# Decay and value-rate mixing factors applied to the low-rank weights, and the opening norm in two groups of two tiles

## What is computed

```python
def rms_norm(x, g):
    y = xf * lax.rsqrt(jnp.mean(xf * xf, axis=-1, keepdims=True) + RMS_EPS)
    return y * g
# hn = rms_norm(h, norm1_g[0]); in rwkv7_time_mix, x is hn:
    xx = token_shift(x) - x
    xs = x[None] + xx[None] * mu[:, None, None, :]
    xr, xw, xk, xv, xa, xg = xs[0], xs[1], xs[2], xs[3], xs[4], xs[5]
    rkv = jnp.einsum('nbtc,ncd->nbtd', jnp.stack([xr, xk, xv]), w_rkv)
    w = -jax.nn.softplus(-(w0 + jnp.tanh(xw @ w1) @ w2)) - 0.5
    a = jax.nn.sigmoid(a0 + (xa @ a1) @ a2)
    g = jax.nn.sigmoid(xg @ g1) @ g2
```

## Time before, and how its profile is read

| what | value |
|---|---|
| time, three runs | 1353.4, 1347.73, 1347.72 us, median 1347.73 |
| the profiled execution | 1350.32 us, of which 1347.4 us are the span from first to last instruction |
| PE busy in the span | 1153.2 us (86%) |
| DVE, ACT, POOL busy | 538.5, 382.7, 248.7 us |
| mean granted clock of TensorE | 0.947 of full |

### The profile page before, as it was taken

How to read it: one execution, slowest core, us unless ns; L and a number is a source line. 1 busy time by engine, 2 the same in 40 slices (tenths; PEclk the granted TensorE clock), 3 DMA queues, 4 the chain that set the end, 5 groups by cost and what they waited for, 6 DMA issues and landing times.

```text
span 1347.4 us, 27828 instructions
## 1 busy us (share of the span) xinstructions
PE 1153.2 (86%) x11854; PEld 627.0 (47%) x11854; DVE 538.5 (40%) x951; ACT 382.7 (28%) x727; POOL 248.7 (18%) x250
## 2 busy tenths in 40 slices
PE   5999999999999789899988873999359989997780
PEld 3365555655555544555544432444124545544440
DVE  6845544554555322411111104599961331111114
ACT  3233334333333221111111113455550211111112
POOL 2000000000000001312221110588810422212110
PEclk8999999999999899999999995999679999999996
DMA  5011010110110603799999986126200589999985
GB/s 161 3 54 37 22 49 21 37 35 26 45 37 20 282 2 130 304 359 425 424 424 425 426 334 249 63 89 278 86 4 17 201 320 422 425 426 425 425 345 211
DMA packets 50154, 271.84 MB, mean 202 GB/s; under 512 B 16338, under 2 KB 19538, under 8 KB 31600
## 3 DMA queue, kind: packets, MB, share of 16 engines
q1 hardware_dynamic: 38000, 240.67, 44.1%
q0 software_dynamic: 10880, 21.00, 4.1%
q10 hardware_dynamic: 1152, 8.39, 1.6%
HBM read 263.73 MB, written 23.07 MB: 213 GB/s over the span
## 4 chain that ended last, share of the span: by engine, by line
PE 60%; DMA 17%; DVE 9%; POOL 5%; ACT 3%; issue 3%; SPq 2%; POOLq 0%; DVEq 0%; ACTq 0%
PE psum L1228 13%; DMA big<-in_moe_w_gate_up_dram 12%; PE psum L812 10%; PE psum L1703 8%; PE psum L1416 5%; POOL big L1897 5%; PE psum L825 4%; DMA conv_w<-in_moe_w_gate_up_dram 3%; PE psum L1406 2%; DVE psum L1999 2%; PE psum L1917 2%; DVE h L916 2%; SPq L355 1%; PE psum L791 1%; PE psum L457 1%
## 5 line engine op out<-in xcount | busy, mean ns | idle before, releaser
L812 PE MATMUL psum<-big 128*64 128x256 f32 x1728 | 218.0, 396 | 42.3 <-DMA big<-in_moe_w_gate_up_dram 30.8
L1228 PE MATMUL psum<-big 128*128 128x512 f32 x384 | 194.2, 624 | 5.0 <-ACT big L1266 5.0
L812 PEld LDWEIGHTS psum<-big 128*64 128x64 f32 x1728 | 120.7, 141 | 125.0 <-DMA big<-in_moe_w_gate_up_dram 42.3
L887 DVE TENSOR_TENSOR big<-big,psum 128x128 f32<-128x128 f32 x64 | 18.4, 288 | 323.0 <-ACT big L853 323.0
L725 POOL TENSOR_SCALAR big<-big 128x1024 f32<-128x1024 f32 x8 | 22.8, 2848 | 604.6 <-PE psum L457 604.5
L753 POOL DMA_INDIRECT chosen<-big x64 | 63.7, 995 | 346.7 <-ACT big L863 187.8
L825 PE MATMUL psum<-big 128*64 128x512 f32 x512 | 120.8, 593 | 1.2 <-ACT big L858 1.2
L1897 POOL TENSOR_TENSOR big<-big 128x512 f32<-128x512 f32 x88 | 111.8, 1271 | 45.2 <-ACT big L1956 33.7
L1703 PE MATMUL psum<-big 128*128 128x512 f32 x256 | 115.4, 603 | 5.6 <-ACT big L1969 5.6
L1917 PE MATMUL psum<-big,conv_w 128*128 128x512 f32 x256 | 110.4, 593 | 2.2 <-ACT big L415 1.2
L1559 ACT COPY big<-psum 128x512 f32<-128x512 f32 x96 | 57.2, 622 | 141.2 <-PE psum L1416 74.4
(11 more groups left out here) (250 smaller groups left out, 1359.7 us busy)
## 6 DMA issues: line engine op xcount, KB each, us to landing
big<-in_moe_w_gate_up_dram SPq DMA_DIRECT2D x54, 2048.0 KB
big<-in_moe_w_down_dram SPq DMA_DIRECT2D x64, 1024.0 KB, 30.4
conv_w<-in_moe_w_gate_up_dram SPq DMA_DIRECT2D x10, 2048.0 KB
big<-in_rwkv_w_rkv_dram SPq DMA_DIRECT2D x24, 512.0 KB, 3.3
conv_w<-in_conv_w_pw_dram SPq DMA_DIRECT2D x8, 1024.0 KB, 4.8
big<-chosen ACTq DMA_DIRECT2D x8, 1024.0 KB, 8.1
big<-in_rwkv_w_o_dram SPq DMA_DIRECT2D x1, 4096.0 KB, 14.0
rows<-big POOLq DMA_DIRECT2D x8, 512.0 KB, 6.0
```

The costliest lines, as they stand in the source:

```text
L812: last = nc.tensor.matmul(o[half * SLOTS:(half + 1) * SLOTS, 0:F_EXP].rearrange("p (u f) -> p u f", u=2), m.xT[e // 2 % 2][:, c, (e % 2) * ...
L1228: last = nc.tensor.matmul(bank[b], m.w[:, n, c, :], x[:, c, :], start=(c == 0), stop=(c == C - 1))
```

## The change

The copies `xw` and `xa` are no longer made. Since `(hnT + mu*xx) @ w` is `hnT @ w + xx @ (mu*w)` with `mu` along the features, PE multiplies `hnT` with the plain weights and `xx` with weights that POOL has multiplied by `mu` (`lora1_mu`, 16 operations of 128 x 64), into the same banks. The norm takes two groups of two tiles, so L445, L403 and L405 run twice, on two columns each.

```diff
+        TWO_AND_TWO = ((0, TT // 2), (TT // 2, TT))
+        NORM_GROUPS = (TWO_AND_TWO, EACH_TILE, LAST_ALONE, EACH_TILE, LAST_ALONE)
...
-                self.xw = self.yg
-                self.xa = big[:, tiles + 2 * D:tiles + 2 * D + C * T].rearrange("p (c t) -> p c t", t=T)
+                self.lora1_mu = Arena(big, yg_at).take(C, P)
...
+        def pool_rwkv_mixed_weights(m, pool):
+            pool.wait_ge(m.lora_in, 48)
+            pool.wait_ge(m.params_in, 16 * m.n_params)
+            for c in range(C):
+                for n, at in ((1, 0), (4, 64)):
+                    nc.gpsimd.tensor_scalar(m.lora1_mu[:, c, at:at + 64], m.lora1[:, c, at:at + 64], m.mu[:, n, c:c + 1],
+                                            None, ALU.mult).then_inc(m.lora1_mixed, 1)
...
         def pe_rwkv_hidden(m, pe):
             pe.wait_ge(m.lora_in, 48)
+            pe.wait_ge(m.hnT_ready.sem, m.hnT_ready.by(2 * TT))
             for c in range(C):
-                pe.wait_ge(m.lerped, lerped(1, c))
-                hw = nc.tensor.matmul(bank[2][0:64], m.lora1[:, c, 0:64], m.xw[:, c, :], start=(c == 0), stop=(c == C - 1))
-                pe.wait_ge(m.lerped, lerped(4, c))
-                ha = nc.tensor.matmul(bank[3][64:P], m.lora1[:, c, 64:P], m.xa[:, c, :], start=(c == 0), stop=(c == C - 1))
+                nc.tensor.matmul(bank[2][0:64], m.lora1[:, c, 0:64], m.hnT[:, c, :], start=(c == 0), stop=False)
+                nc.tensor.matmul(bank[3][64:P], m.lora1[:, c, 64:P], m.hnT[:, c, :], start=(c == 0), stop=False)
+            pe.wait_ge(m.xx_ready, TT + 1)
+            pe.wait_ge(m.lora1_mixed, 2 * C)
+            for c in range(C):
+                hw = nc.tensor.matmul(bank[2][0:64], m.lora1_mu[:, c, 0:64], m.xx[:, c, :], start=False, stop=(c == C - 1))
+                ha = nc.tensor.matmul(bank[3][64:P], m.lora1_mu[:, c, 64:P], m.xx[:, c, :], start=False,
+                                      stop=(c == C - 1))
...
         def dve_rwkv(m, dve):
-            dve_norm(m, dve, lambda t: dve.wait_ge(h_in[t], 16), ALL_TILES)
+            dve_norm(m, dve, lambda t: dve.wait_ge(h_in[t], 16), TWO_AND_TWO)
             dve_rwkv_differences(m, dve)
             dve.wait_ge(m.params_in, 16 * m.n_params)
-            for c in range(C):
-                dve_rwkv_lerp(m, dve, m.xw, 1, c)
-                dve_rwkv_lerp(m, dve, m.xa, 4, c)
```

More of the change, by code:

```diff
@@ L155, in bass_hybrid_rwkv7_conformer_hmoe @@
         LAST_ALONE = ((0, TT - 1), (TT - 1, TT))
-        ALL_TILES = ((0, TT),)
-        NORM_GROUPS = (ALL_TILES, EACH_TILE, LAST_ALONE, EACH_TILE, LAST_ALONE)
+        TWO_AND_TWO = ((0, TT // 2), (TT // 2, TT))
+        NORM_GROUPS = (TWO_AND_TWO, EACH_TILE, LAST_ALONE, EACH_TILE, LAST_ALONE)
         norm_squares = sem("norm_squares")
@@ L1018, in __init__ @@
                     "mixed").split())
-                self.xx_ready, self.lerped = sem("rwkv_xx_ready"), sem("rwkv_lerped")
+                self.xx_ready, self.lerped, self.lora1_mixed = sem("rwkv_xx_ready"), sem("rwkv_lerped"), sem("rwkv_lora1_mixed")
                 (self.hw_in_psum, self.ha_in_psum, self.hg_in_psum) = signals(sem("rwkv_hidden_in_psum"), 3)
@@ L1146, in sp_rwkv @@
             sp.dma_start(m.wo, a["rwkv_w_o"][i].rearrange("(q p) d -> p q d", p=P)).then_inc(m.wo_in, 16)
-        LERPED = {n: (at, step) for n, at, step in ((1, 1, 2), (4, 2, 2), (5, 2 * C + 1, 1), (2, 3 * C + 1, 1),
-                                                    (0, 4 * C + 1, 1), (3, 5 * C + 1, 1))}
+        LERP_ORDER = (5, 2, 0, 3)
         def lerped(n, c):
-            at, step = LERPED[n]
-            return at + step * c
+            return C * LERP_ORDER.index(n) + c + 1
+        def pool_rwkv_mixed_weights(m, pool):
[5 more added lines that the diff above has]
+                                            None, ALU.mult).then_inc(m.lora1_mixed, 1)
         def dve_rwkv_differences(m, dve):
             dve.wait_ge(m.hnT_ready.sem, m.hnT_ready.by(2))
-            nc.vector.tensor_scalar(m.xx[:, :, 0:1], m.hnT[:, :, 0:1], -1.0, None, ALU.mult)
+            nc.vector.tensor_scalar(m.xx[:, :, 0:1], m.hnT[:, :, 0:1], -1.0, None, ALU.mult).then_inc(m.xx_ready, 1)
             for t in range(TT):
@@ L1163, in dve_rwkv_differences @@
                                         ALU.subtract).then_inc(m.xx_ready, 1)
-            dve.wait_ge(m.xx_ready, TT)
+            dve.wait_ge(m.xx_ready, TT + 1)
         def dve_rwkv_lerp(m, dve, out_, n, c):
@@ L1767, in act_rwkv @@
         def act_rwkv(m, act):
-            act_norm(m, act, lambda t: act.wait_ge(h_in[t], 16), ALL_TILES)
+            act_norm(m, act, lambda t: act.wait_ge(h_in[t], 16), TWO_AND_TWO)
             act_rwkv_hidden(m, act)
@@ L2095, in _ @@
             pool_rwkv_masks(rw, pool)
+            pool_rwkv_mixed_weights(rw, pool)
             pool_moe(moe[0], pool)
```

## The result

| kernel | median us (lowest to highest) | runs | profiled execution, its span | mean clock |
|---|---|---|---|---|
| before | 1349.88 (1347.72 to 1353.4) | 6 | 1350.32, 1347.4 | 0.947 |
| after | 1362.21 (1357.22 to 1365.17) | 6 | 1364.22, 1362.5 | 0.943 |

After over before is 1.0089, 95% interval 1.0063 to 1.0114: 12.3 us slower at the medians, 15.1 us between the two profiled spans. The forecast was 1347.5 us, range 1344.5 to 1350.5. Two things happened. One lies in the opening and is the mechanism of the third rival, with a wait of 3.4 us where that rival said 12.5. The other lies behind the opening, in the work on the pairs of heads (70 to 585 us), in code that the change doesn't touch, and was not among the rivals.

What follows compares the result with a forecast made beforehand. PE was taken to bound the changed opening: 19.5 + 0.1 + 13.8 gives 33.4 us (32.9 without the stretch) against 33.44, a gain taken as 0.2, so span 1347.2 and median 1347.5 us, range 1344.5 to 1350.5.

Steps and rivals of the forecast that it cites:

- the third rival: Opening: POOL's 16 operations each wait for a 1.22 us DVE operation, 24.6 us in all; PE waits 12.5; 1360 us; chance 0.03.
- The arrival of `hnT`: Opening norm: first scaling waits for `params_in`, two groups bring 0.35 us, stretched DVE work puts the last copy at 19.5.
- PE's 13.8 us: Opening, before L1191: 16 chunks of two 0.43 us steps at full clock take PE 13.8 us after the last `hnT`.
- the loss of DVE's 10.7 us: Opening: DVE loses 16 mixes, 10.7 us, but almost nothing of it arrives because PE's added work takes its place.
- I take them as hidden: Opening: POOL's 16 weight products, 14.3 to 20.5 us, end before PE needs them at 26.4, behind PE's first half.
- not free for DVE: Opening: beside POOL, DVE's last scaling is stretched by 1.6 and the differences lose up to 2 us more.
- the rows agree for DVE and not for POOL: Shared SBUF port: the earlier profile was read as DVE being slowed beside POOL while POOL's L725 stays at 2.84 to 2.86 us.
- The threshold given: Opening: POOL's 16 operations may cost 0.75 us each before PE feels them at its second half.
- The clock: Opening: PE's 13.8 us run at full clock, since the idle stretch after the transposes shrinks from 4.4 us to about 1.2.
- What follows runs as before, only shifted: Everything behind the start of L1181: unchanged apart from a shift, so only that start, 33.44 to 33.51 before, counts.

## Why the prediction was wrong

- **The arrival of `hnT`, right.** The first scaling is bound by `params_in` (9.90 us, behind `mu`), the two groups alone bring nothing (0.9995). L1179 starts at 18.85 where 19.6 was said: the first scaling started 0.2 us sooner than said (9.90, not 10.1), and DVE was not stretched, which the prediction had put at 0.5.
- **PE's 13.8 us and the loss of DVE's 10.7 us, right.** With the weights on DVE the two halves take 13.9 us and L1191 starts at 33.39. Removing 16 mixes gains nothing, as said.
- **"I take them as hidden", "not free for DVE", wrong.** The step failed where L725's constant 2.85 us was read as "POOL is never held up". In the earlier trace rows POOL starts first, 531.95 against 532.18, and DVE pays; the same holds in each of the four places where L553 runs beside L725, and beside the other four L725 no DVE operation with two SBUF inputs runs. Those rows show who pays when POOL is first; they say nothing on POOL arriving second, so "the rows agree for DVE and not for POOL" was read from cases that could not tell. In the opening DVE runs one two-input operation behind the other, so POOL is second nearly each time and gets in once per mix and once per two differences, 14.68 us in all. It was the third rival, given 0.03. Its mechanism was right. Its price, 24.6 us for POOL and 12.5 for PE, was too high, since it charged each operation a DVE operation of 1.22 us; only two stood beside the differences at 2.4 us each, ten beside mixes (the first 0.89, then 0.73 each). PE waits 3.4 us. The threshold given, 0.75 us each, was nearly right: with POOL starting at 14.48 and PE's first half ending at 25.93 it is 0.72, and 0.92 is over it.
- **The clock, right for the first half, and for the second only under that condition.** The first half is at full clock from 18.85. Behind the wait for POOL it was low from 28.7 to 35.5 and cost another 2.9 us. L1179 at 18.85 plus the 13.9 us of the run without POOL's part would put L1191 at 32.75, 0.7 before the 33.44 of the kernel before; it starts at 39.28. So the wait and the clock cost 6.5 us in the opening, which is the delay of 5.85 against before, and 1.7 come back with the low stretch that vanished at 44.6.
- **"What follows runs as before, only shifted", wrong, and the larger part.** The prediction had counted the added PE instructions as time in their own stage. They also move every later PE instruction by 65 in its block of 256. That costs 9 to 10 us of the 12.3, as 65 increments in the kernel before show (1.0071), and as 191 more instructions in the changed kernel take back (1.0089 to 1.0020).

What is shown is that the count of PE instructions ahead of a run of small matmuls changes the time, that 256 more bring time and places back, and that PE halts at one remainder. That the halt is a wait for the packet of instructions is argued from its size, from there being one for each block, and from its end 1.2 to 1.5 us before PE goes on at all 28 halts; it wasn't tried by itself. Also open are what sets off a packet, what brings the low clock behind some halts, and the run with 32 instructions.

## What to carry to other kernels

Before giving POOL work beside DVE, look at what DVE's operations read: beside two SBUF inputs a POOL operation got through only about once per DVE operation here (0.73 us beside mixes, 2.4 beside differences), beside a PSUM input it ran at 0.41 us. When a change alters the number of PE instructions ahead of a long, tightly issued part, time the old kernel with as many instructions that do nothing: here that control alone moved it by 0.7%, and without it the loss would have been laid on the change's own work. A wait on PE is to be priced with the clock behind it, 3.4 us of waiting and 2.9 us of low clock here, and the price is to be read some way behind, since 1.7 us of it came back.

## What was not expected of the hardware

- PE halts for 0.3 to 1.9 us within the pairs (up to 5 us at the last one) at one place in 256 of its instructions, in the pairs where 64 x 64 matmuls follow one another closely. Adding 65, 128 or 192 instructions cost 0.7 to 0.8%, 224 or 256 nothing.
- A semaphore increment on PE takes 0.15 us when many stand in a row; 191 of them put off the first transposes by 18.9 us.
- With 95 small matmuls ahead of the transposes the clock stayed high across a wait of 3.01 us at L1184, where the changed kernel without them fell after 3.38 us. Whether the matmuls or the shorter wait did this isn't shown.
